# Order of PSUM banks and operand halves in the matmuls of a two-layer decoder trunk

## The reference

```python
def swiglu(x, w_gu, w_down):
    a, b = jnp.split(x @ w_gu, 2, axis=-1)
    return (jax.nn.silu(a) * b) @ w_down

for i in range(DEPTH):                       # DEPTH = 2
    x = layer_norm(ALPHA * x + 0.5 * swiglu(x, ffn1_w_gu[i], ffn1_w_down[i]), ...)
    if i % 2 == 0: y, qm = gla_mix(x @ gla_w_in[j], ...)      # gated linear attention
    else:          y, qm = conv_mix(x @ conv_w_in[j], ...)    # 31-tap depthwise convolution
    m = mem_attention(qm, mem, mem_w_kv[i])
    x = layer_norm(ALPHA * x + jnp.concatenate([y, m], axis=-1) @ w_out, ...)
    x = layer_norm(ALPHA * x + 0.5 * swiglu(x, ffn2_w_gu[i], ffn2_w_down[i]), ...)
```

## Time and profile before

| | |
|---|---|
| device time, median of 3 runs | 2279.32 us (2277.9 to 2279.92) |
| span of the profiled execution, from its first to its last instruction | 2278.2 us |
| instructions | 24232, of them 9608 matmuls |
| TensorE busy | 2163.0 us, 95% of the span |
| mean granted TensorE clock | 0.967 of full speed |
| VectorE, ScalarE, GpSimd busy | 36%, 31%, 41% |

### The profile page before, as it was taken

How to read it: one execution, slowest core, us unless ns; L and a number is a source line. 1 busy time by engine, 2 the same in 40 slices (tenths; PEclk the granted TensorE clock), 3 DMA queues, 4 the chain that set the end, 5 groups by cost and what they waited for, 6 DMA issues and landing times.

```text
span 2278.2 us, 24232 instructions
## 1 busy us (share of the span) xinstructions
PE 2163.0 (95%) x9608; PEld 1748.7 (77%) x9608; DVE 830.9 (36%) x963; ACT 697.3 (31%) x900; POOL 944.2 (41%) x295
## 2 busy tenths in 40 slices
PE   7999999999899999999999999998587899999998
PEld 7888888678777788887868888776465577888886
DVE  2233221424425432331142332125499753332213
ACT  5322222364313322222232222224145333222222
POOL 3244433443122444443344443436776234444342
PEclk9999999999989999999999999999798799999999
DMA  6422222232102223222322222232110122223221
GB/s 207 166 92 92 94 84 95 70 111 82 48 19 91 76 96 106 92 78 88 111 71 96 92 92 83 89 106 75 56 37 7 49 93 74 92 92 98 83 91 60
DMA packets 191706, 195.62 MB, mean 86 GB/s; under 512 B 3567, under 2 KB 190061, under 8 KB 191388
## 3 DMA queue, kind: packets, MB, share of 16 engines
q1 hardware_dynamic: 191036, 192.62, 26.0%
q10 hardware_dynamic: 608, 2.13, 0.2%
HBM read 190.54 MB, written 4.19 MB: 85 GB/s over the span
## 4 chain that ended last, share of the span: by engine, by line
PE 85%; DVE 5%; POOL 4%; ACT 3%; issue 1%; DMA 1%; DVEq 0%; POOLq 0%; ACTq 0%
PE bank L1231 26%; PE bank L1233 26%; PE bank L1232 26%; POOL wlo L314 3%; PE bank L1306 1%; DVE u L1173 1%; POOL xlo L324 1%; ACT u L543 1%; PE bank L1576 1%; ACT whi L479 1%; DMA raw<-in_mem_w_kv_dram 1%; PE bank L1332 1%; DVE scratch L895 1%; DVE scratch L956 0%; PE bank L1570 0%
## 5 line engine op out<-in xcount | busy, mean ns | idle before, releaser
L314 POOL TENSOR_TENSOR wlo<-raw,whi 128x2048 fp32r<-128x2048 f32 (+2 forms) x184 | 786.6, 4275 | 1155.9 <-ACT whi L479 1155.9
L1231 PE MATMUL bank<-xhi,whi 128*128 128x512 f32 x1712 | 673.4, 393 | 35.9 <-POOL wlo L314 35.9
L479 ACT CAST whi<-raw 128x2048 fp32r<-128x2048 f32 (+2 forms) x202 | 341.5, 1690 | 1194.4 <-PE bank L1233 1157.8
L1233 PE MATMUL bank<-xhi,wlo 128*128 128x512 f32 x1712 | 669.9, 391 | 0.0
L1232 PE MATMUL bank<-xlo,whi 128*128 128x512 f32 x1712 | 669.9, 391 | 0.0
L1231 PEld LDWEIGHTS bank<-xhi,whi 128*128 128x128 f32 x1712 | 323.6, 189 | 105.8 <-issue 37.8
L1233 PEld LDWEIGHTS bank<-xhi,wlo 128*128 128x128 f32 x1712 | 323.3, 189 | 67.7
L1232 PEld LDWEIGHTS bank<-xlo,whi 128*128 128x128 f32 x1712 | 323.7, 189 | 67.3 <-issue 0.5
L877 DVE TENSOR_TENSOR scratch<-scratch,bank 128x512 f32<-128x512 f32 x88 | 56.5, 684 | 631.5 <-PE bank L1233 631.5
L1231 PE MATMUL bank<-h_hi,whi 128*128 128x512 f32 x704 | 281.0, 399 | 0.1
L1233 PE MATMUL bank<-h_hi,wlo 128*128 128x512 f32 x704 | 278.5, 396 | 0.0
(11 more groups left out here) (235 smaller groups left out, 1913.8 us busy)
## 6 DMA issues: line engine op xcount, KB each, us to landing
raw<-in_ffn_w_gu_dram SPq DMA_DIRECT2D x88, 1024.0 KB, 5.0
raw<-in_ffn_w_down_dram SPq DMA_DIRECT2D x48, 768.0 KB, 4.4
raw<-in_gla_w_in_dram SPq DMA_DIRECT2D x13, 1024.0 KB, 5.3
raw<-in_conv_w_in_dram SPq DMA_DIRECT2D x10, 1024.0 KB, 5.0
raw<-in_mem_w_kv_dram SPq DMA_DIRECT2D x8, 1024.0 KB, 6.6
raw<-in_ffn_w_down_dram SPq DMA_DIRECT2D x16, 512.0 KB, 3.4
raw<-in_gla_w_out_dram SPq DMA_DIRECT2D x4, 1024.0 KB, 5.2
raw<-in_conv_w_out_dram SPq DMA_DIRECT2D x4, 1024.0 KB, 5.1
```

Source lines behind the costliest of these rows:

```text
L314: nc.gpsimd.tensor_tensor(wlo[:, s, 0:kc, 0:width], raw[:, s, 0:kc, 0:width], whi[:, s, 0:kc, 0:width].bitcast(F32), ALU.subtract).then_in ...
L479: nc.scalar.copy(whi[:, s, 0:kc, 0:width], raw[:, s, 0:kc, 0:width]).then_inc(hi_ready, 1)
L1231: nc.tensor.matmul(to, whi[:, s, k, w], hi, start=start, stop=False)
L1233: return nc.tensor.matmul(to, wlo[:, s, k, w], hi, start=False, stop=stop)
```

## The change

The new `mm3_in_turn` takes two banks and, for one k, issues six matmuls in turn: high weights by high data to either bank, low weights by high data to either bank, high weights by low data to either bank. `chunk`, `out_a`, the memory projection and the diagonal convolution chunks use it; `by_halves` alternates banks too; `mm3` itself now does its product with the low data last. `down_pair` and `out_b` use it except at the very end of pair 3, where the last 4 k-blocks stay one bank after the other. `y_even` now comes one matmul before the pair's end. Down pairs 0 and 2 use banks 0 and 1, pairs 1 and 3 banks 2 and 3. The loops over pairs 1 and 2 are written out on TensorE and VectorE.

```diff
             def residual_ffn(ln, n0):
-                residual_pair(ln, 0, n0 + 4, 0.5)
-                with dve.Fori(1, 3) as p:
-                    residual_pair(ln, p, n0 + 4 * p + 4, 0.5)
-                residual_pair(ln, 3, n0 + 16, 0.5, last=True)
+                for p in range(4):
+                    residual_pair(ln, p, n0 + 4 * p + 4, 0.5, b0=2 * (p % 2), last=p == 3)
...
+            def mm3_in_turn(tos, s, k, his, los, start, stop):
+
+                for n, (half, xs) in enumerate(((whi, his), (wlo, his), (whi, los))):
+                    last = [nc.tensor.matmul(to, half[:, s, k, t * P:t * P + P], xs[t], start=(start and n == 0),
+                                             stop=(stop and n == 2)) for t, to in enumerate(tos)]
+                return last
...
                     for k in range(DK):
-                        for t, b in enumerate(banks):
-                            last = mm3(bank[b][:, :], s, k, t, xhi[:, k, :], xlo[:, k, :], k == 0, k == DK - 1)
+                        last = mm3_in_turn([bank[b][:, :] for b in banks], s, k, [xhi[:, k, :]] * 2, [xlo[:, k, :]] * 2,
+                                           k == 0, k == DK - 1)[-1]
...
-                        for t, b in enumerate(banks):
-                            for half in (whi, wlo):
+                        for half in (whi, wlo):
+                            for t, b in enumerate(banks):
...
-                    for t in range(2):
-                        if c == 0 and not (first and p == 0):
-                            pe.wait_ge(y_evac, 8 * ln + 2 * p - 1 + t)
+                    elif p >= 2 and c == 0:
+                        pe.wait_ge(y_evac, 8 * ln + 2 * (p - 2) + 2)
+                    if p == 3 and c == len(DOWN_K) - 1:
+                        for t in range(2):
+                            for k in range(k0, k0 + kc):
+                                if t == 1 and k == FK - 1:
+                                    sums_u(ln)
+                                last = mm3(to[t], c % 2, k - k0, t, h_hi[:, k, :], h_lo[:, k, :], False, k == FK - 1)
+                            last.then_inc(w_used if t else y_even, 1)
+                    else:
                         for k in range(k0, k0 + kc):
-                            if first and p == 3 and t == 1 and k == FK - 1:
-                                sums_u(ln)
-                            last = mm3(bank[t][:, :], c % 2, k - k0, t, h_hi[:, k, :], h_lo[:, k, :], k == 0, k == FK - 1)
-                        if t == 1:
-                            last.then_inc(w_used, 1)
-                        elif c == len(DOWN_K) - 1:
-                            last.then_inc(y_even, 1)
+                            even, last = mm3_in_turn(to, c % 2, k - k0, [h_hi[:, k, :]] * 2, [h_lo[:, k, :]] * 2,
+                                                     k == 0, k == FK - 1)
+                        if c == len(DOWN_K) - 1:
+                            even.then_inc(y_even, 1)
+                        last.then_inc(w_used, 1)
...
+                to = [bank[b0][:, :], bank[b0 + 1][:, :]]
+                together = B_K - 4 if p == 3 else B_K
+                for k in range(together):
+                    if p == 0:
+                        pe.wait_ge(y_done, k + 1)
+                    even, last = mm3_in_turn(to, p % 2, k, [y_h[:, k, :]] * 2, [y_l[:, k, :]] * 2, False, k == B_K - 1)
+                if p < 3:
+                    even.then_inc(y_even, 1)
+                    last.then_inc(w_used, 1)
+                    return
```

More of the change, by code:

```diff
@@ L1231, in mm3 @@
                 nc.tensor.matmul(to, whi[:, s, k, w], hi, start=start, stop=False)
-                nc.tensor.matmul(to, whi[:, s, k, w], lo, start=False, stop=False)
-                return nc.tensor.matmul(to, wlo[:, s, k, w], hi, start=False, stop=stop)
+                nc.tensor.matmul(to, wlo[:, s, k, w], hi, start=False, stop=False)
+                return nc.tensor.matmul(to, whi[:, s, k, w], lo, start=False, stop=stop)
+            def mm3_in_turn(tos, s, k, his, los, start, stop):
[3 more added lines that the diff above has]
+                return last
             def chunk(n, s, banks, ready=None):
@@ L1275, in down_pair @@
             def down_pair(f, p):
-                ln, n = LN_FFN[f], FFN_N[f] + FK + 4 * p
-                first = isinstance(p, int)
+                ln, n, b0 = LN_FFN[f], FFN_N[f] + FK + 4 * p, 2 * (p % 2)
+                to = [bank[b0][:, :], bank[b0 + 1][:, :]]
                 k0 = 0
@@ L1281, in down_pair @@
                     pe.wait_ge(lo_ready, n + c + 1)
-                    if first and p == 0:
+                    if p == 0:
                         pe.wait_ge(h_done, FK * f + k0 + kc)
@@ L1344, in ffn @@
                 shift_sum(LN_FFN[f])
-                with pe.Fori(1, 3) as p:
+                for p in range(1, 4):
                     down_pair(f, p)
-                down_pair(f, 3)
                 stats(LN_FFN[f], (GLA_N, FFN_N[2], CONV_N, None)[f])
@@ L1356, in out_a @@
                     pe.wait_ge(y_evac, 8 * ln + 2 * (p - 2) + 2)
-                for t in range(2):
-                    for k in range(A_K):
-                        last = mm3(bank[b0 + t][:, :], p % 2, k, t, mo_hi[:, k, :], mo_lo[:, k, :], k == 0, False)
+                for k in range(A_K):
+                    last = mm3_in_turn([bank[b0][:, :], bank[b0 + 1][:, :]], p % 2, k, [mo_hi[:, k, :]] * 2,
+                                       [mo_lo[:, k, :]] * 2, k == 0, False)[-1]
                 last.then_inc(w_used, 1)
@@ L1368, in out_b @@
                     return
+                to = [bank[b0][:, :], bank[b0 + 1][:, :]]
+                together = B_K - 4 if p == 3 else B_K
+                for k in range(together):
+                    if p == 0:
+                        pe.wait_ge(y_done, k + 1)
[4 more added lines that the diff above has]
+                    return
                 for t in range(2):
[L1370 to L1373, removed]
+                    for k in range(together, B_K):
+                        if t == 1 and k == B_K - 1:
                             sums_u(ln)
-                        last = mm3(bank[b0 + t][:, :], p % 2, k, t, y_h[:, k, :], y_l[:, k, :], False, k == B_K - 1)
+                        last = mm3(to[t], p % 2, k, t, y_h[:, k, :], y_l[:, k, :], False, k == B_K - 1)
                     last.then_inc(w_used if t else y_even, 1)
@@ L1452, in _ @@
                         pe.wait_ge(mem_ready, k + 1)
-                    for t in range(2):
-                        last = mm3(bank[2 * (n % 2) + t][:, 0:NMEM], n % 2, k, t, mem_hi[:, k, :], mem_lo[:, k, :], k == 0, k == DK - 1)
+                    last = mm3_in_turn([bank[2 * (n % 2) + t][:, 0:NMEM] for t in range(2)], n % 2, k, [mem_hi[:, k, :]] * 2,
+                                       [mem_lo[:, k, :]] * 2, k == 0, k == DK - 1)[-1]
                 last.then_inc(w_used, 1)
@@ L1619, in diag_chunk @@
                     tap = 8 * g + j
-                    for t in range(2):
-                        last = mm3(bank[2 + t][:, :], g % 2, j, t, cin_hi[:, t, tap:tap + SEQ], cin_lo[:, t, tap:tap + SEQ],
-                                   tap == 0, tap == WIDTH - 1)
+                    last = mm3_in_turn([bank[2][:, :], bank[3][:, :]], g % 2, j, [cin_hi[:, t, tap:tap + SEQ] for t in range(2)],
+                                       [cin_lo[:, t, tap:tap + SEQ] for t in range(2)], tap == 0, tap == WIDTH - 1)[-1]
                 last.then_inc(w_used, 1)
```

## The result

| | before | after |
|---|---|---|
| device time, median | 2279.62 us (2277.9 to 2280.45, 4 runs) | 2306.56 us (2305.11 to 2311.65, 4 runs) |
| span of the profiled execution | 2278.2 us | 2303.1 us |
| mean granted TensorE clock | 0.967 | 0.966 |

The ratio after to before is 1.0113, with a 95% interval from 1.0098 to 1.0129: the change costs 27 us. The forecast was 2286, and its range ended at 2302.

What follows compares the result with a forecast made beforehand. TensorE was taken to bound the kernel, by its matmul pace and its waits. Losses of 22.4 us against a gain of 16.0 turned the 2278.2 us span into 2284.6, giving a forecast of 2286 us, range 2251 to 2302.

Steps and rivals of the forecast that it cites:

- the pace of single-bank stretches: Matmuls on h in down pairs and output projections: expected to start every 0.2267 us in the new order instead of 0.2333.
- 16.0 us of gain: Down pairs 13.4 us, gated output projection 1.8, convolution's 0.6 and 0.2, all from the faster pace; x gains nothing.
- no change of pace: Rival: h is slow because of where it lies, not its bank; no gain, 2298 us; chance 0.27.
- (a): shift_sum after pair 0, four SwiGLUs and gated layer: 0.78 us late in five new places, 3.9 us.
- (b): Second chunk after down pairs 1 and 2: TensorE waits 1.06 us eight times, 8.5 us; 0.82 each at old pace.
- (c): Second chunk after pair 0, already 0.2 us late: a faster first chunk only waits longer, giving back 1.0 us.
- (d): Output projections before out_a 3: second evacuation later, TensorE waits 2.9 us, 5.8 for two layers.
- (e): After out_b 2: GpSimd's later split meets VectorE's block 6 sum, sums_u 1.6 us later, 3.2 for two layers.
- The waits don't come: Rival: pace as forecast, but VectorE's and ScalarE's chain is shorter or has slack; 2263 us; chance 0.12.
- the rival's 19.0 us: Losses from waits at the old pace, without any gain: 3.9 + 6.6 + 5.5 + 3.0 us.
- the clock falls: Rival: TensorE's clock drops after two of four waits in the output projections, 10 us more, 2296; chance 0.09.
- Every matmul gets faster: Rival: staying in a bank costs 20 ns; x alone gains 68 us, about 2217, or half, 2251; chance 0.15.

Runs made afterwards that it cites:

- e3: Changed kernel, but the last four k-blocks of every pair go bank by bank, so y_even comes 12 matmuls before the end; 2280.03 us, ratio 1.0004.
- e4: Kernel before, with the new order (mm3_in_turn) in chunk alone; 2281.78 us, ratio 1.0002.
- e16: e3 with e7's placing: new order except in each pair's last four k-blocks, all tiles placed like the weights; 2269.48 us, ratio 0.9949.
- e1: Kernel before, with 64 unused bytes ahead of the region holding h, putting h on the weights' phase; 2267.94 us, ratio 0.9944.
- e5: Kernel before, with 192 unused bytes ahead of the region instead of 64, h 128 bytes off the weights; 2279.53 us, one run.
- e6: Kernel before, with both weight tiles moved by 64 bytes, x and h at their old places modulo 256; 2311.26 us, one run.
- e13: Kernel before, with 320 unused bytes ahead of the region, h 256 bytes off the weights; 2267.14 us, one run.
- e14: Kernel before, with 64 unused bytes ahead of xhi, so all tiles move and none against another; 2279.34 us, one run.
- e2: Changed kernel with the same 64-byte gap as e1; 2300.34 us, ratio 1.0083.
- e7: Kernel before, with e1's gap and 64 bytes behind conv_in, so all three-product tiles start like the weights; 2266.79 us, ratio 0.9944.
- e15: e7 with ScalarE's cast of the next pair's second chunk put between a pair's two squares; 2266.47 us, ratio 0.9939.

## Why the prediction was wrong

**The step that failed is the pace of single-bank stretches, taken at 0.2267.** The prediction read right that h starts every 0.2333 us and x every 0.2267, and it had the decisive doubt: the convolution's output projection, in a single bank, at 0.2286, and x indifferent to the order. From these two rows it concluded that "the bank isn't all that matters", where they allow the plainer reading that for x and h it doesn't matter at all. The 16.0 us of gain were a hope set against a row. They are 0 (e3, e4, e16). What sets the pace of x and h is the start of the moving tile against that of the weights (e1, e5, e6, e13, e14). The rival "no change of pace" named this cause and had 0.27; it should have had most of the chance. Of the 20.6 us between 2286 and the measured 2306.56 this step makes 12.6: the gain of 16.0, less 3.4 because at the old pace the waits are shorter.

**The waits came as worked out**, at the old pace:

| | predicted | measured |
|---|---|---|
| (a) `shift_sum` late | 0.78 | 0.79 |
| (b) second chunk after pairs 1 and 2 | 0.82 | 0.98 to 1.01 |
| (c) second chunk after pair 0 | 0.2, as before | 0.2, as before |
| (d) `out_a` 3 | 2.75 | 2.67 and 2.69 |
| (e) `sums_u` later | 1.5 | 1.47 and 1.56 |

The chain behind them is as told: one engine's fixed order (squares, then cast) carries a late evacuation on to GpSimd and from there to TensorE. "The waits don't come" was wrong, and e3 shows that without the late `y_even` none of the new waits is there.

**Two terms are missing from the rival's 19.0 us.** Some 0.1 us behind each of 13 new waits (`shift_sum` and second chunks), because the pace is not at once back (1.3 us). And what follows (d) and (e), 9.5 us, up to 8.5 of it half clock. The prediction had this as a rival of its own, "the clock falls", for two of the four waits and 10 us. It set it against "no change of pace" as if only one of them could come. Both came: 2298 + 10 = 2308, against 2306.56 measured. That this sum comes so near is in part luck: the down and output projections account for 31 us between the spans, and 6.2 us came back in other stages. The two rivals together are why the time lies beyond the range: its upper end of 2302 was near one rival's time, and not at that of two together.

**"Every matmul gets faster"** is refuted by e4 and by the changed kernel: 0.2267 on x, full alternation or not. The Trainium skill's 215.8 ns for a warm distance of 512 columns (the same page and section as above) was reached in no run here, in any order or place; 226.7 ns was the least mean of any family. What the skill says of banks cycled each iteration (the same page, A second HAM failure mode: psum-queue depth-cycling) this trace doesn't bear out either: the clock was 1.00 from 100 to 300 and from 311 to 337, with the bank changed at every start.

Left open: why the offset matters, and why c at its two places follows the order. The runs show by how much, for one size of matmul. Whether any of the 5.0 us by which the convolution stage was shorter than before belongs to the change was not tried by itself.

## What to carry to other kernels

When two families of equal matmuls differ in pace, list everything in which they differ, addresses too, and change that one thing in the unchanged kernel before a loop is rewritten for it: 16 floats of padding gave the 0.6% that the reordering could not. An order that makes a first result late is paid at every reader in turn, so follow it to the engine whose program puts an unrelated cast behind that result. And a wait of 2.9 us on TensorE had a second price here, 1.6 us in the clock, which belongs in the same sum and not in a case of its own.

## What the runs showed of the hardware

- **The pace of an fp32r matmul of 128x128 by 128x512 depends on where its moving tile starts against its weight tile, modulo 256 bytes**, at full clock, where high and low data lie alike (mean distances of a family):

| moving start minus weight start | distance | seen in |
|---|---|---|
| 0 (and 256) | 226.7 to 227.1 ns, small families to 227.6 | x in all but e6; h in e1, e2, e7, e13, e15, e16; the convolution's `mo` and c in e7, e15, e16 |
| +64 | 229.1 to 229.3 ns | the convolution's `mo` in e5 and e6 |
| 128 | 232.2 to 233.1 ns | h and y in e5 and e6; the convolution's `mo` before and in e3, e4 |
| -64 (and 192) | 233.2 to 233.4 ns | h before and after; x in e6; the convolution's `mo` in e1 and e13 |

  Bank order, and the order of high and low halves, changed the means of h and x, with the most matmuls, by no more than 0.1 ns. In the changed kernel single distances of y alternate between 231.0 and 235.4, with the mean of 233.3 that y had before. c, whose high and low tiles lie 64 bytes apart, doesn't fit the table: 230.3 to 230.9 ns in the old order, 231.9 and 232.1 in the new.
- **A VectorE addition on 128x512 fp32 with both inputs in SBUF that starts beside GpSimd's split is held past the split's end**: 0.69 us alone, 2.51, 3.57 and 4.67 beside splits of 4.64, 3.50 and 4.61 us, and each ends 0.55 us after its split. An operation with one input in a PSUM bank is not held: before, L934 starts at 759.34 within the split of 756.97 to 761.62 and takes 0.69 us.
- **The clock fell behind waits, not behind bank changes**: 3.4 us at 1.2 GHz after a distance of 2.9 us, none after those of 1.2 us in the down pairs. After the 1.70 us before `sums_u`, with the norm behind it, it fell for 13.7 us; without that wait it fell in the same norm too, for 6.8.
- **The first distance after a wait is some 0.1 us longer** than those that follow: 0.34 instead of 0.23 us behind the second chunk's wait, 0.53 instead of 0.43 for the ones matmuls.
